# Last down projection: 14 of 44 pairs of contraction tiles as seven block products of sums

## The reference

```
u = h @ w_up
c = causal convolution of width 3 over u, with bias
gate, val = split(c)
x = x + (silu(gate) * val) @ w_down      # (256, 5632) @ (5632, 2048)
```

## Time and profile before

| what | us |
|---|---|
| three runs, without the profiler | 2217.39, 2217.53, 2218.05 |
| median of these | 2217.53 |
| the profiled execution, first to last instruction (its span) | 2216.0 |
| last down projection in it, first transpose to DVE's last copy | 243.0 |
| from there to the end of the span | 3.3 |

### The profile page before, as it was taken

One profiled execution on the slowest core, in us unless ns is written; L12 is line 12 of the kernel. 1 busy time (PEld: TensorE's weight loads), 2 busy tenths in 40 slices (PEclk: granted clock), 3 DMA queues, 4 the chain that ended last, 5 costly groups with the idle time before them and its releaser, 6 DMA issues.

```text
span 2216.0 us, 34772 instructions
## 1 busy us (share of the span) xinstructions
PE 2209.4 (100%) x12470; PEld 1935.2 (87%) x12470; DVE 1484.4 (67%) x1753; ACT 1177.3 (53%) x1409; POOL 14.3 (1%) x21
## 2 busy tenths in 40 slices
PE   9999999999999999999999999999999999999999
PEld 8888898888888888888899888888888888888887
DVE  7666556677777777555578888667777777774443
ACT  7565555555555555444455466555555555553333
POOL 0000000000000000000010000000000000000000
PEclk9999999999999999999999999999999999999999
DMA  7555555555555555565566544555555656566664
GB/s 270 166 168 177 171 162 181 195 185 190 189 193 186 189 190 191 190 190 189 191 212 198 177 157 139 161 183 191 182 198 181 194 184 198 180 193 201 201 199 136
DMA packets 113829, 411.55 MB, mean 186 GB/s; under 512 B 12769, under 2 KB 13537, under 8 KB 113761
## 3 DMA queue, kind: packets, MB, share of 16 engines
q1 hardware_dynamic: 112320, 406.70, 56.5%
q10 hardware_dynamic: 1008, 2.30, 0.3%
q0 software_dynamic: 432, 1.57, 0.2%
HBM read 408.42 MB, written 2.10 MB: 185 GB/s over the span
## 4 chain that ended last, share of the span: by engine, by line
PE 99%; DMA 0%; SPq 0%; DVE 0%; ACT 0%; issue 0%; DVEq 0%
PE psum L1301 99%; DMA raw<-w_all 0%; PE psum L1621 0%; PE psum L1557 0%; DVE w_lo L747 0%; ACT w_hi L289 0%; SPq L237 0%; SPq L235 0%; DVE upad L822 0%; SPq L236 0%; SPq L234 0%; DVEq L83 0%
## 5 line engine op out<-in xcount | busy, mean ns | idle before, releaser
L747 DVE TENSOR_TENSOR w_lo<-raw,w_hi 128x1024 fp32r<-128x1024 f32 x769 | 935.6, 1224 | 678.6 <-ACT w_hi L289 672.8
L1301 PE MATMUL psum<-xg,w_hi 128*128 128x512 f32 (+1 forms) x3936 | 1358.3, 392 | 1.9 <-DVE w_lo L747 1.0
L289 ACT CAST w_hi<-raw 128x1024 fp32r<-128x1024 f32 x770 | 803.1, 1049 | 771.4 <-PE psum L1301 767.6
L1301 PE MATMUL psum<-xg,w_lo 128*128 128x256 f32 (+1 forms) x3920 | 1090.8, 278 | 0.0
L1301 PEld LDWEIGHTS psum<-xg,w_hi 128*128 128x128 f32 x3936 | 736.0, 187 | 156.7 <-issue 2.2
L1301 PEld LDWEIGHTS psum<-xg,w_lo 128*128 128x128 f32 x3920 | 742.6, 189 | 2.6 <-issue 2.2
L1301 PE MATMUL psum<-hid,w_hi 128*128 128x512 f32 x704 | 244.1, 391 | 0.0
L1301 PE MATMUL psum<-w_hi,hid 128*128 128x512 f32 x704 | 217.9, 390 | 0.0
L1301 PE MATMUL psum<-hid,w_lo 128*128 128x256 f32 x704 | 197.4, 280 | 0.0
L1301 PE MATMUL psum<-att,w_hi 128*128 128x512 f32 x512 | 178.8, 393 | 0.0
L1301 PEld LDWEIGHTS psum<-hid,w_hi 128*128 128x128 f32 x704 | 131.7, 187 | 28.6
(11 more groups left out here) (176 smaller groups left out, 1062.9 us busy)
## 6 DMA issues: line engine op xcount, KB each, us to landing
raw<-w_all SPq DMA_DIRECT2D x770, 512.0 KB, 3.8
xres<-x_in SPq DMA_DIRECT2D x3, 512.0 KB, 9.0
cst<-consts_in ACTq DMA_DIRECT2D x2, 768.0 KB, 6.6
raw<-w_all SPq DMA_DIRECT2D x2, 256.0 KB, 3.6
xres<-x_in SPq DMA_DIRECT2D x2, 256.0 KB, 3.8
out_t<-part POOLq DMA_DIRECT2D x1, 512.0 KB, 7.3
out_t<-conv POOLq DMA_DIRECT2D x1, 512.0 KB, 7.4
out_t<-gates POOLq DMA_DIRECT2D x1, 512.0 KB, 7.0
```

What stands on the lines that cost most here:

```text
L289: act.copy(w_hi[:, c % RING, :], raw[:, c % RING, :]).then_inc(hi_ready, 1)
L747: dve.tensor_tensor(w_lo[:, c % RING, :], raw[:, c % RING, :], f32(w_hi[:, c % RING, :]), ALU.subtract).then_inc(lo_ready, 1)
L1301: return pe.matmul(o, lhsT, rhs, start=start, stop=True, skip_group_check=True)
```

## The change

The contraction tiles are taken in pairs, and the output columns in two halves of 1024. One *step* is one pair by one half: blocks of 2 contraction tiles by 2 column halves of 512 (four weight blocks, in two pieces of the stream), against 2 token halves by 2 contraction tiles of `hid` (four activation blocks). A plain step makes the 2 x 2 x 2 = 8 block products as before, into banks 0 to 3. A marked step makes 7 products of sums of blocks, into banks 0 to 3 directly where that is possible and into banks 4 to 7 otherwise; these four are added to the results at the end of each half. 6 of 22 steps in the first half and 8 of 22 in the second are marked, with one or two plain steps between two of them.

For a marked step DVE adds and subtracts the four raw weight blocks (`weight_sums`), and four blocks of the ring are split in place of two (512, 1024, 1024 and 1024 columns), so that ACT makes four casts and DVE four lows. Both pieces are given back to SP together, with the last low. The sums of activation blocks are needed for 8 pairs, and are the same in both column halves; DVE makes them in the first half (`y_combine`, `y_low`) and ACT makes their high parts (`y_high`), into `xg`, which is free by then.

The stores change: each of the eight results (2 token halves by 4 blocks of 512 columns) is one final add on DVE (`final`) and one store of 256 KB, five from POOL, two from SP, the last in two halves of 128 KB from SP and ACT. ACT's three copies out of PSUM fall away. The stream of this layer's `w_down` is laid out anew on the host (`_down_pairs`), with as many pieces as before.

The core of the diff:

```diff
+KINDS = ("CCCCCCCSCSCCSCSCCSCSCC",
+         "SCCSCSCCSCSCCSCSCCSCCC")
+Y_PAIRS = (7, 9, 12, 14, 17, 19, 1, 3)
+Y_AT = {5: 0, 6: 1, 8: 2, 11: 3, 14: 4, 15: 5, 17: 6, 18: 7}
+DRAIN_AT = [KINDS[g].rindex("S") + 1 for g in range(2)]
...
 POOL
+            for n in range(5):
+                g, j = n // 4, n % 4
+                _, o, th, m = FINALS[j]
+                pool.wait_ge(fin, n + 1)
+                pool.dma_start(out_tok[:, th, PIECE * g + m * HALF:PIECE * g + (m + 1) * HALF], o).then_inc(stored, 16)
...
 ACT
+            def high(piece, slot, half=slice(0, PIECE)):
+                act.wait_ge(raw_full[piece % RING], 16 * (piece // RING + 1))
+                act.wait_ge(piece_used, slot - RING + 1)
+                act.copy(w_hi[:, slot % RING, half], raw[:, piece % RING, half]).then_inc(hi_ready, 1)
+            def high_sums(n, made, src, slot):
+                act.wait_ge(made, n + 1)
+                act.wait_ge(piece_used, slot - RING + 1)
+                act.copy(w_hi[:, slot % RING, :], src).then_inc(hi_ready, 1)
+            def y_high(y):
+                act.wait_ge(y_terms, y + 1)
...
+                act.copy(xg[:, 2 * y:2 * y + 2, 0:T], y_buf[y % 2][:, M2].rearrange("p (k t) -> p k t", k=2)).then_inc(y_hi, 1)
+            def out_tokens():
+                for st in STEPS[5:]:
+                    if st.g == 0 and st.pos in Y_AT:
+                        y_high(Y_AT[st.pos])
+                    if st.seven:
+                        high(st.piece, st.slot, M2)
+                        high_sums(st.of, t13_ready, conv_f, st.slot + 1)
+                        high_sums(st.of, t24_ready, gates_f, st.slot + 2)
+                        high(st.piece + 1, st.slot + 3)
+                    else:
+                        if st.piece >= L1_DN + 11:
+                            high(st.piece, st.slot)
+                        high(st.piece + 1, st.slot + 1)
+                    if st.pos == DRAIN_AT[st.g]:
+                        drain(st.g)
...
 DVE
+            def weight_sums(st):
+                a, b = st.piece % RING, (st.piece + 1) % RING
+                for c in (st.piece, st.piece + 1):
+                    dve.wait_ge(raw_full[c % RING], 16 * (c // RING + 1))
+                if b == a + 1:
+                    dve.tensor_tensor(conv[:, :, :].rearrange("p (n h) t -> p n (h t)", n=2), raw[:, a:a + 2, M2],
+                                      raw[:, a, M1].unsqueeze(1).to_broadcast([P, 2, HALF]), ALU.add).then_inc(t13_ready, 1)
+                else:
+                    dve.tensor_tensor(conv_f[:, M1], raw[:, a, M2], raw[:, a, M1], ALU.add)
+                    dve.tensor_tensor(conv_f[:, M2], raw[:, b, M2], raw[:, a, M1], ALU.add).then_inc(t13_ready, 1)
+                dve.wait_ge(t13_ready, st.of + 1)
+                dve.tensor_tensor(gates_f[:, M1], conv_f[:, M1], raw[:, b, M2], ALU.add).then_inc(t2_ready, 1)
+                dve.wait_ge(t2_ready, st.of + 1)
+                dve.tensor_tensor(gates_f[:, M2], gates_f[:, M1], raw[:, b, M1], ALU.add).then_inc(t24_ready, 1)
+            def out_tokens():
...
+                for st in STEPS[5:]:
+                    y = Y_AT.get(st.pos) if st.g == 0 else None
+                    a, b = st.piece % RING, (st.piece + 1) % RING
+                    if y is not None:
+                        y_combine(y)
+                    if st.seven:
+                        weight_sums(st)
+                        low(raw[:, a, M2], st.slot, M2, seven_lo)
+                        low(conv_f, st.slot + 1, slice(0, PIECE), seven_lo)
+                        if st.g and st.pos == 0:
+                            for j in range(4):
+                                final(0, j, end[0])
+                        low(gates_f, st.slot + 2, slice(0, PIECE), seven_lo)
+                        low(raw[:, b, :], st.slot + 3, slice(0, PIECE), lo_ready, 2)
+                    else:
+                        if st.piece >= L1_DN + 11:
+                            low(raw[:, a, :], st.slot, slice(0, PIECE), lo_ready)
+                        low(raw[:, b, :], st.slot + 1, slice(0, PIECE), lo_ready)
+                    if y is not None:
+                        y_low(y)
+                    if st.pos == DRAIN_AT[st.g]:
+                        drain(st.g)
+                for j in range(4):
+                    final(1, j, end[1])
...
 PE
+            def seven(st):
...
+                pe.wait_ge(seven_lo, 3 * st.of + 1)
...
+                three(psum[:, 4, :], hid, k, 0, st.slot, M2, first).then_inc(piece_used, 1)
+                pe.wait_ge(seven_lo, 3 * st.of + 2)
+                pe.wait_ge(y_ready, y + 1)
+                three(psum[:, 5, :], xg, 2 * y, 1, st.slot + 1, M1, first)
+                three(psum[:, 6, :], xg, 2 * y, 0, st.slot + 1, M2, first).then_inc(piece_used, 1)
+                pe.wait_ge(seven_lo, 3 * st.of + 3)
+                last = three(psum[:, 7, :], xg, 2 * y + 1, 0, st.slot + 2, M1, first)
...
+                three(psum[:, 2, :], hid, k + 1, 1, st.slot + 2, M2).then_inc(piece_used, 1)
+                pe.wait_ge(lo_ready, st.piece + 2)
...
+                three(psum[:, 0, :], hid, k + 1, 0, st.slot + 3, M1)
...
+                three(psum[:, 1, :], xg, 2 * y + 1, 1, st.slot + 3, M2).then_inc(piece_used, 1)
```

More of the change, by code:

```diff
@@ L72, with __init__, down_steps @@
 NV = V_DSA + 3
+L1_DN = NPIECES - DN
+DUO = FF // 256
+KINDS = ("CCCCCCCSCSCCSCSCCSCSCC",
+         "SCCSCSCCSCSCCSCSCCSCCC")
+Y_PAIRS = (7, 9, 12, 14, 17, 19, 1, 3)
+class Step:
+    def __init__(self, g, pos, pair, piece, slot, seven, of):
+        self.g, self.pos, self.pair, self.piece, self.slot = g, pos, pair, piece, slot
+        self.seven, self.of = seven, of
+def down_steps():
+    steps, piece, slot, of = [], L1_DN, L1_DN, 0
+    for g in range(2):
+        sevens = iter(Y_PAIRS if g else sorted(Y_PAIRS[:KINDS[0].count("S")]))
+        rest = iter([p for p in range(DUO) if g == 0 or p not in Y_PAIRS])
+        for pos, kind in enumerate(KINDS[g]):
+            pair = pos if g == 0 else next(sevens) if kind == "S" else next(rest)
+            steps.append(Step(g, pos, pair, piece, slot, kind == "S", of))
+            piece, slot, of = piece + 2, slot + (4 if kind == "S" else 2), of + (kind == "S")
+    return steps
+STEPS = down_steps()
+DRAIN_AT = [KINDS[g].rindex("S") + 1 for g in range(2)]
+Y_AT = {5: 0, 6: 1, 8: 2, 11: 3, 14: 4, 15: 5, 17: 6, 18: 7}
 C_TRI, C_ONE, C_AVG, C_ID, C_SBM, C_CM, C_COS, C_SIN = 0, 128, 256, 384, 512, 640, 1024, 1280
@@ L577, in mlp_layer @@
                 else:
[L578 to L591, removed]
+                    out_tokens()
@@ L811, in out_groups, with low @@
                         add_group(4 * (m - 1) + g, g, 4 * (g % 2))
[L813 to L820, removed]
-                    for n in range(2):
-                        dve.tensor_copy(upad[:, 2 * th + n, 0:T], psum[:, 6 + th, n * T:(n + 1) * T]).then_inc(tail_ready, 1)
+            def low(src, slot, half, done, n=1):
+                dve.wait_ge(hi_ready, slot + 1)
+                dve.tensor_tensor(w_lo[:, slot % RING, half], src, f32(w_hi[:, slot % RING, half]), ALU.subtract).then_inc(done, n)
@@ new lines, in final @@
+            def final(g, j, slots_used):
+                bank, o, _, _ = FINALS[j]
+                if j < 3:
+                    dve.wait_ge(bank_done, 3 * g + j + 1)
+                else:
+                    dve.wait_ge(piece_used, slots_used)
+                if j == 0:
+                    dve.wait_ge(t_made, g + 1)
+                    dve.wait_ge(drained, g + 1)
+                if g and j == 3:
+                    for n in range(2):
+                        c = slice(n * T, (n + 1) * T)
+                        dve.tensor_tensor(o[:, c], psum[:, bank, c], o[:, c], ALU.add).then_inc(fin, 1)
+                else:
+                    dve.tensor_tensor(o, psum[:, bank, :], o, ALU.add if j else ALU.subtract).then_inc(fin, 1)
@@ new lines, in out_tokens @@
+            def out_tokens():
+                dve.wait_ge(h_ready, 2 * UPG)
+                end = [st.slot + 2 for st in STEPS if st.pos == DUO - 1]
+                for st in STEPS[5:]:
[12 more added lines that the diff above has]
+                        low(raw[:, b, :], st.slot + 3, slice(0, PIECE), lo_ready, 2)
+                    else:
+                        if st.piece >= L1_DN + 11:
[7 more added lines that the diff above has]
+                    final(1, j, end[1])
@@ L1545, in mlp_layer, with three @@
                 else:
-                    out_tokens(base + UP)
-            def out_tokens(base):
-                per = FT // 2
+                    out_tokens()
+            def three(acc, src, k, th, slot, half, new=False):
+                x_hi, x_lo = src[:, k, th * P:(th + 1) * P], src[:, k, T + th * P:T + (th + 1) * P]
+                mm(acc, x_hi, w_hi[:, slot % RING, half], new)
+                mm(acc, x_hi, w_lo[:, slot % RING, half])
```

(39 more changed lines are left out.)

101 lines of the change are left out of this document (89 added, 12 removed).

## The result

The changed kernel takes 2232.54 us (median of five runs, 2231.28 to 2234.46) against 2217.53 before (2217.33 to 2218.07): a ratio of 1.0068, interval 1.0056 to 1.0080. It is 15.0 us slower. The direction was forecast, the size was not: 2223.1 was the forecast, and the range ended at 2230.5.

A forecast was written before the change was run, and what follows sets the result against it. TensorE (PE), busy throughout the last down projection, was taken as the bound. Terms −9.5 + 0.3 + 9.0 + 5.0 + 0.8 = +5.6 us gave 2223.1 us, matmuls saved being more than paid back by PE's waits; range 2217 to 2230.5.

The forecast's parts named there:

- 42 matmuls fewer: In 14 marked steps, 21 matmuls each in place of 24, at 0.2267 us a matmul: −9.5 us.
- first new wait: Plain steps 8, 15, 18 of the first half: PE waits as token sums precede lows and casts; 2.5, 3.4, 3.1, together +9.0.
- second new wait: Marked steps one plain step behind another (first half 14; second half 5, 10, 15) wait on late second loads: 1.25 each, +5.0.
- the turn: Between column halves, four final adds precede the third low of the second half's first step: +0.8 us, between 0.2 and 2.0.
- the clock: Granted clock taken to stay at 1.00 throughout the last down projection, so no term for it in the sum.
- transposes; what is left over: First matmul after transposes lasts 0.48 instead of 0.39; three more such places make +0.3 us.
- landed at 2.57 + 0.17 + 0.59 + 4.2: In the second wait: last low's end, SP's issue, second issue, its load time; second piece lands at 7.53 us.
- the rival with 0.04: Clock falls to 1.2 GHz after the three long waits, doubling the next plain step's 5.44 us: about 2239; chance 0.04.
- the prediction's own sign of being wrong: Among signs against the forecast in the last down projection's trace: a granted clock under 1.00.
- Slow pairs: Rival: a pair's second load takes 5.4 to 6.6 us, four waits grow by 1.2 to 2.4: 2228 to 2233; chance 0.13.
- the end: Kernel's end: two 256-column adds replace two copies, and POOL's fifth store lands 0 to 0.6 us later; taken as 0.

The follow-up runs named there:

- Experiment 2: Against the changed kernel, the eight token sums are moved so that none is ahead of a plain step behind a marked one; 2227.66 us, ratio 1.0040.
- experiment 5: Against the changed kernel, only ACT's y_high is put behind its step's casts, DVE's order as it was; 2225.05 us, ratio 1.0033.
- experiment 6: Against the changed kernel, only three marked steps and two token sums, the rest of the new order kept; 2216.30 us, ratio 0.9994.
- experiment 7: Against the changed kernel, seven marked steps in the second half, two plain steps between any two, one pair's token sums dropped; 2225.79 us, ratio 1.0038.
- experiment 4: Against the changed kernel, DVE makes lows of only 16 of 1024 columns of the two blocks of sums in marked steps; 2228.57 us, ratio 1.0046.
- experiment 8: Against the kernel before, eight or nine useless dependent DVE additions stand ahead of five of its lows; 2243.48 us in one run.
- experiment 1: Against the changed kernel, a marked step gives its first raw piece back with its first block's low, not the last; 2221.84 us, ratio 1.0021.

## Why the prediction was right or wrong

By the terms of its sum, against the profiled execution (PE's last matmul ends 13.5 us later than before):

| term | forecast | measured |
|---|---|---|
| 42 matmuls fewer | −9.5 | −9.5 |
| first new wait, steps 8, 15, 18 | +9.0 | 2.58 + 3.31 + 3.19 = 9.1 |
| second new wait, short step two after another | +5.0 | 2.09 + 1.23 + 2.11 + 1.56, and 0.33 at step 13: 7.3 |
| the turn | +0.8 | 1.2 |
| the clock | 0 | 2 × 7 × 0.2 = 2.8 |
| transposes; what is left over | +0.3 | 2.6 |
| sum | +5.6 | +13.5 |

That the medians differ by 15.0 and not by 13.5 is mostly that the profiled run of the changed kernel is its fastest, 1.3 us under its median.

Three terms failed, each by two to three us: the second new wait was too small (5.0, measured 7.3), the clock stood at 0 (2.8), and what is left over, mostly what comes with each wait and fall, had hardly a term (2.6 against +0.3). The range ended 13.0 above the kernel before, so with any one of the three right the median would have lain inside it.

- **First new wait: right**, in place, mechanism and size (forecast 2.5, 3.4, 3.1). The 128x128 sums, bounded from afar, took 0.29 on average, as forecast. Experiment 2 takes the wait away with the sums, and experiment 5 takes 1.7 us of it by ACT's order alone.
- **Second new wait: mechanism right, size wrong.** The step that failed is "landed at 2.57 + 0.17 + 0.59 + 4.2". The pair of the earlier trace rows was one within SP's loop body, and 4.2 was the lower end of the earlier trace rows. Where the pair straddles the loop's end, the 0.59 is 0.87. The landings were 4.74, 4.27, 4.80 and 4.47 (two are shown above, the others and step 13's below). With these, and 0.06 for the split first sum in the two straddling steps (14 and 10), the forecast 1.25 each becomes 2.13, 1.32, 2.19 and 1.52, against the measured 2.09, 1.23, 2.11 and 1.56: the clock count held for each pair's sum, its inputs didn't (within a pair the second wait is 0.3, not 0.5). Step 13's 0.33 was missed: it hangs on the last of four loads issued within 2.7 us, which took 6.8.

```profile
2041.89 4.74 DMA raw<-w_all
...
2166.41 6.79 DMA raw<-w_all
...
2180.75 4.47 DMA raw<-w_all
```

- **The clock: the rival with 0.04 came true in part**, and the prediction's own sign of being wrong, a granted clock under 1.00, is in the rows. The term was put at 0. My reason against it was the idle place of the earlier trace rows, 1.0 us long, which says nothing of waits three times as long. Its price was wrong too: not 5.4 us after each of three waits, but 1.4 after two of them. The Trainium skill (TensorE: Matmul & The Clock Gate, Part 1) says that an idle array is put at half rate; the traces agree for the waits behind which the clock fell, at 6 to 8 matmuls mostly, and show other waits behind which it didn't.
- **The turn**: DVE was still in the first of its four final adds when PE was through with bank 3 (about 2102.1) and began its nine prepared matmuls; 1.2 lies within the 0.2 to 2.0 given, and 0.8 was too kind.
- **The left over 2.6** was hardly in the sum. The second matmul behind a wait starts 0.31 to 0.34 us after the first, not 0.227: 13 places, 1.3 in all. Four pitches at the edges of the two falls lie between the two levels (0.4), the whole stretch starts 0.3 later, and the rest is spread thin. The +0.3 was itself miscounted: five first matmuls stand behind transposes, against four before, so one is new and not three, 0.1.
- **Slow pairs** (0.13) was nearer than the forecast, at 2228 to 2233, but not for its reason: landings stayed under its 5.4 in all four places, and the clock and the left over made up the number. That it came nearer is luck.
- **Costed at nothing, rightly:** the end. From the start of DVE's last operation to the end of the span it is 3.3 us in both kernels, and experiment 6 finds no price for the new frame.

That the change's time spreads over 3.2 us, against 0.7 before, fits a number of falls and landings that differs between runs. Only one run of it left a trace, so for the slower ones this is argued and not shown.

## What to carry to other kernels

An engine's queue is served in order, so work that only a later step needs must stand behind the casts and lows that keep PE's ring full; and a buffer shared by several readers is given back with its last read, not with the last operation of the step. A wait of PE can cost more than its length, since the clock may fall behind it: here removing two kinds of wait together brought 4 us more than their sum, and the falls went with them. A duration for a load that is issued behind another comes from a loaded stretch, and the loop's end in the issuing queue belongs in it.

## What was not expected of the hardware

- **Whether the clock falls after a wait isn't told by the wait's length alone.** It fell after 3.31 and 3.19 (the change), 2.85 + 0.28 and 2.58 (experiment 7), and 2.75, 2.48, 2.03 + 0.34 and 1.62 + 0.28 (experiment 2). It didn't fall after 2.58 (the change), 3.05 (experiment 4), 2.29 (experiment 8) and 1.66 + 0.28 (experiment 5). What else decides is open.
- **A second load close behind another landed after 4.2 to 5.9 us** (mean 4.67 over 14 pairs of the change), the first after 3.2 to 4.4, though the DMA engines were busy for half of the stretch. Where four loads followed within 2.7 us, the third and the fourth landed after 5.4 to 6.8. With pieces given back apart (experiment 1) the mean of all loads fell from 4.61 to 4.18. The Trainium skill (DMA: Bandwidth & Descriptors, Queues, rings and completion order) says that each DMA engine takes a ring's descriptors in order; the traces agree in that the second took longer than the first in all 14 pairs. That it waits for the first on engines that they share is argued and not shown.
